# x's causal convolution taken in token rows instead of channel columns, in a hybrid Mamba-2 and attention layer

## The reference, cut to what matters

```
def causal_depthwise_conv(u, w, b):
    k = w.shape[0]
    out = lax.conv_general_dilated(u, w[:, None, :], (1,), padding=[(k - 1, 0)], feature_group_count=u.shape[-1])
    return out + b

xbc = silu(causal_depthwise_conv(xbc, conv_w, conv_b))
xs, Bm, Cm = split(xbc)
y = ssd_chunked(xs, dt, A, Bm, Cm)
y = y + d_skip * xs
y = group_rms_norm(y * silu(z)) * norm_w
```

## Time and profile before

| | |
|---|---|
| median of three runs | 2049.8 us |
| profiled execution: its time | 2051.72 us |
| profiled execution: span, first to last instruction | 2050.1 us |
| busy share: TensorE, VectorE, ScalarE, GpSimd | 100%, 76%, 57%, 8% |
| DMA traffic | 419.80 MB, 205 GB/s mean |

### The profile page before, as it was taken

One profiled execution on the slowest core, in us unless ns is written; L12 is line 12 of the kernel. 1 busy time (PEld: TensorE's weight loads), 2 busy tenths in 40 slices (PEclk: granted clock), 3 DMA queues, 4 the chain that ended last, 5 costly groups with the idle time before them and its releaser, 6 DMA issues.

```text
span 2050.1 us, 28075 instructions
## 1 busy us (share of the span) xinstructions
PE 2040.8 (100%) x9580; PEld 1677.7 (82%) x9580; DVE 1566.3 (76%) x1861; ACT 1172.0 (57%) x1496; POOL 171.6 (8%) x195
## 2 busy tenths in 40 slices
PE   9999999999999999999999999999999999999999
PEld 8888877778888888888888888888888888887887
DVE  6777866665856777777667887888898889877866
ACT  5444655555556666666655554556666666645543
POOL 1121000000011222222000000010000000000000
PEclk9999999999999999999999999999999999999999
DMA  7656675654566666666565657598888888667574
GB/s 250 199 182 203 188 220 166 176 162 152 182 204 186 185 185 184 185 190 187 167 192 183 212 168 238 177 307 244 258 254 237 250 259 250 196 205 232 176 246 154
DMA packets 220626, 419.80 MB, mean 205 GB/s; under 512 B 16449, under 2 KB 22002, under 8 KB 220290
## 3 DMA queue, kind: packets, MB, share of 16 engines
q1 hardware_dynamic: 212162, 399.48, 61.8%
q0 software_dynamic: 7776, 18.94, 4.4%
q10 hardware_dynamic: 608, 0.34, 0.1%
HBM read 410.25 MB, written 4.26 MB: 202 GB/s over the span
## 4 chain that ended last, share of the span: by engine, by line
PE 92%; DVE 3%; DMA 2%; ACT 1%; issue 0%; SPq 0%; DVEq 0%; ACTq 0%
PE acc L2246 72%; PE side L2333 8%; PE acc L2333 6%; PE side L2262 3%; DMA w_raw<-in_w_ffn_down 1%; DVE w_lo L2038 1%; PE side L2402 1%; PE side L2549 1%; DVE w_raw L1953 0%; ACT w_hi L1216 0%; DVE w_lo L1257 0%; DMA x_row<-in_x 0%; DMA w_raw<-in_w_in 0%; PE acc L2262 0%; ACT w_hi L724 0%
## 5 line engine op out<-in xcount | busy, mean ns | idle before, releaser
L1257 DVE TENSOR_TENSOR w_lo<-w_raw,w_hi 128x1024 fp32r<-128x1024 f32 x332 | 420.7, 1280 | 245.7 <-ACT w_hi L724 244.5
L724 ACT ACTIVATE w_hi<-w_raw 128x1024 fp32r<-128x1024 f32 x332 | 348.5, 1057 | 355.7 <-PE acc L2246 315.2
L2246 PE MATMUL acc<-w_hi,h_hi 128*128 128x512 f32 x1248 | 498.7, 400 | 0.2
L2246 PE MATMUL acc<-w_hi,h_lo 128*128 128x512 f32 x1248 | 487.0, 390 | 0.0
L2246 PE MATMUL acc<-w_lo,h_hi 128*128 128x512 f32 x1248 | 485.9, 389 | 0.0
L2246 PEld LDWEIGHTS acc<-w_hi,h_hi 128*128 128x128 f32 x1248 | 234.4, 188 | 52.7 <-issue 7.0
L2246 PEld LDWEIGHTS acc<-w_hi,h_lo 128*128 128x128 f32 x1248 | 234.3, 188 | 50.3
L2246 PEld LDWEIGHTS acc<-w_lo,h_hi 128*128 128x128 f32 x1248 | 234.7, 188 | 47.6 <-issue 1.9
L1932 DVE TENSOR_TENSOR w_lo<-w_raw,w_hi 128x1024 fp32r<-128x1024 f32 x136 | 165.1, 1220 | 38.0 <-ACT w_hi L1137 35.4
L1053 ACT ACTIVATE w_hi<-w_raw 128x1024 fp32r<-128x1024 f32 x110 | 116.6, 1061 | 117.2 <-PE acc L2246 70.2
L1137 ACT ACTIVATE w_hi<-w_raw 128x1024 fp32r<-128x1024 f32 x136 | 142.9, 1057 | 65.8 <-PE acc L2246 50.4
(11 more groups left out here) (436 smaller groups left out, 3445.9 us busy)
## 6 DMA issues: line engine op xcount, KB each, us to landing
w_raw<-in_w_in SPq DMA_DIRECT2D x320, 512.0 KB, 4.3
w_raw<-in_w_ffn_down SPq DMA_DIRECT2D x88, 512.0 KB, 4.9
w_raw<-in_w_ffn_gate SPq DMA_DIRECT2D x68, 512.0 KB, 4.6
w_raw<-in_w_ffn_up SPq DMA_DIRECT2D x68, 512.0 KB, 5.2
w_raw<-in_w_ssm_proj SPq DMA_DIRECT2D x64, 512.0 KB, 4.4
side_raw<-in_w_ffn_up SPq DMA_DIRECT2D x40, 512.0 KB, 4.7
w_raw<-in_w_attn_proj SPq DMA_DIRECT2D x32, 512.0 KB, 3.7
w_raw<-in_w_out SPq DMA_DIRECT2D x32, 512.0 KB, 4.7
```

What stands on the lines that cost most here:

```text
L724: nc.scalar.activation(w_hi[:, r], w_raw[:, n % RING], ACT.Copy).then_inc(hi_ready, 1)
L1257: nc.vector.tensor_tensor(w_lo[:, r], w_raw[:, n % RING], w_hi[:, r].bitcast(F32), ALU.subtract).then_inc(lo_ready, 1)
L2246: done = nc.tensor.matmul(acc[p][:, t], a[:, k0 + kk, cut], w[:, r, kk], start=first and kk == n == 0, stop=last and kk == UK - 1 and n == ...
```

## The change

x stays in token rows. SyncE copies `x_proj` three times inside SBUF, shifted by one, two and three partitions (tokens), into `earlier[0..2]`; of each, a second small copy carries the one, two or three tokens that cross from the first token tile to the second. These six copies are issued ahead of the load of z7. GpSimd loads the group's taps and bias, broadcast to all partitions (1 MB and 256 KB). VectorE multiplies four tiles by taps (after z6 and z7), adds them and the bias (after x0' and x1'), ScalarE does the SiLU in place after x2', and VectorE computes `xdt` and `xdt_end` after x4' of the next x chunk. TensorE's sixteen transposes per group and ScalarE's four first taps and `y_row` copy are gone. `y_products` moves from after x1' to after x2', `y_rows` from after x3' to after x4', the scaling of `y_row` moves from VectorE to ScalarE, `exps` to ScalarE's steps 4 and 5, the d_skip product stands behind the loads of the next group on GpSimd and reads `x_proj`.

```diff
         x_proj = at("x_proj", 187, [P, TT, CW])
-        conv_x = at("conv_x", 191, [P, CT, T])
+        earlier = [at(f"earlier{n + 1}", kb, [P, TT, CW]) for n, kb in enumerate((138, 142, 175))]
+        taps_b = at("taps_b", 167, [P, TAPS, CW])
...
+                for u in range(UPC):
+                    if u == UPC - 1:
+                        sp.wait_ge(x_rows_ready, i + 1)
+                        for back in range(1, TAPS):
+                            sp.dma_start(earlier[back - 1][back:P], x_proj[0:P - back]).then_inc(shift_in, 16)
+                            sp.dma_start(earlier[back - 1][0:back, 1], x_proj[P - back:P, 0]).then_inc(shift_in, 16)
+                    load(w_in, u * UK, (i + i) * (CW // 2) + COL_Z)
             with repeat(sp, 2, [(unit, 2 * UPC)]) as i:
                 for c in range(2):
...
+                act.wait_ge(conv_ready, g + 1)
+                nc.scalar.activation(x_proj[:], x_proj[:], ACT.Silu).then_inc(xs_ready, 1)
+            def tail_normed(g):
+                act.wait_ge(y_rstd, g + 1)
+                for t in range(TT):
+                    last = nc.scalar.activation(y_row[:, t], y_row[:, t], ACT.Copy, scale=y_scale[:, t:t + 1])
+                last.then_inc(y_ready, 1)
             def tail_columns(g):
...
+                    act.wait_ge(xdt_ready, g)
+                    act.wait_ge(skip_ready, g)
                 for t in range(TT):
                     last = nc.scalar.activation(x_proj[:, t], acc[0][:, t], ACT.Copy, scale=x_rstd[:, t:t + 1])
                 last.then_inc(x_rows_ready, 1)
+                act.wait_ge(x_rows_ready, g + 1)
+                nc.scalar.sem_inc(acc_free[0], 1)
             def exps(g, hf, head):
                 act.wait_ge(acs_masked, g * 2 + (hf + 1))
+                if hf == 0:
+                    act.wait_ge(taps_read, g + 1)
                 if hf == 0 and not head:
...
-                        act.wait_ge(x_T, g + 1)
-                        for n in range(CT):
-                            last = conv_first_taps(sums(0)[:, n], g * CT, conv_x[:, n], n)
-                        last.then_inc(conv_first, 1)
                     if u == 1:
                         act.wait_ge(cb_sum, g + 1)
                         nc.scalar.activation(cb[:], side[:, 0, 0:3 * P], ACT.Copy).then_inc(cb_ready, 1)
-                    if u == 2:
-                        act.wait_ge(conv_done, g + 1)
-                        nc.scalar.activation(conv_x[:], conv_x[:], ACT.Silu).then_inc(xs_ready, 1)
-                        exps(g, 0, head)
-                    if u == 3:
-                        exps(g, 1, head)
-                    if u == 5:
-                        act.wait_ge(xdt_ready, g + 1)
-                        nc.scalar.activation(y_row[:], side[:, 2:4], ACT.Copy).then_inc(xrow_ready, 1)
+                    if u == 0 and not head:
+                        tail_normed(g - 1)
+                    if u in (4, 5):
+                        exps(g, u - 4, head)
+                    if u == 6:
+                        conv_silu(g)
                 chunk_done()
...
+            def by_taps(tile, back):
+                return nc.vector.tensor_tensor(tile[:], tile[:], taps_b[:, TAPS - 1 - back].unsqueeze(1).broadcast_to([P, TT, CW]), ALU.mult)
+            def conv_step(g, u):
+                if u == 2:
+                    dve.wait_ge(shift_in, g * 96 + 96)
+                    dve.wait_ge(taps_in, g * 32 + 32)
+                    by_taps(earlier[0], 1)
+                    by_taps(earlier[1], 2)
+                if u == 3:
+                    by_taps(earlier[2], 3)
+                    by_taps(x_proj, 0).then_inc(taps_read, 1)
+                if u == 4:
+                    dve.wait_ge(taps_read, g + 1)
+                    nc.vector.tensor_tensor(earlier[0][:], earlier[0][:], earlier[1][:], ALU.add)
+                    link(nc.vector.tensor_tensor(x_proj[:], x_proj[:], earlier[2][:], ALU.add))
+                if u == 5:
+                    link(nc.vector.tensor_tensor(x_proj[:], x_proj[:], earlier[0][:], ALU.add))
+                    nc.vector.tensor_tensor(x_proj[:], x_proj[:], conv_bias_b[:].broadcast_to([P, TT, CW]), ALU.add).then_inc(conv_ready, 1)
+            def x_scaled(g):
                 by_head = "p (h d) -> p h d"
+                dve.wait_ge(xs_ready, g + 1)
+                for t in range(TT):
+                    last = nc.vector.tensor_tensor(
+                        xdt[:, t].rearrange(by_head, d=HP), x_proj[:, t].rearrange(by_head, d=HP),
+                        dt[:, t, bass.ds(g * HG, HG)].unsqueeze(2).broadcast_to([P, HG, HP]), ALU.mult)
+                last.then_inc(xdt_ready, 1)
+                dve.wait_ge(xdt_ready, g + 1)
+                nc.vector.tensor_tensor(
+                    xdt_end[:].rearrange(by_head, d=HP), xdt[:, 0].rearrange(by_head, d=HP),
+                    edge[:, 0, bass.ds(g * HG, HG)].unsqueeze(2).broadcast_to([P, HG, HP]), ALU.mult).then_inc(xdt_end_ready, 1)
+            def tail_step(g, u):
+                if u == 0:
+                    x_scaled(g)
+                if u == 4:
+                    tail_gated(g)
+            def x_chunk(g, head):
                 for u in range(UPC):
                     split_lo()
-                    if u == 0:
-                        dve.wait_ge(conv_first, g + 1)
-                        for back in range(1, TAPS):
-                            conv_taps(g, back)
-                    if u == 1 and not head:
+                    if not head:
+                        tail_step(g - 1, u)
+            def z_chunk(g, head):
+                for u in range(UPC):
+                    split_lo()
+                    if u == 2 and not head:
                         tail_transposed(g - 1)
-                    if u == 2:
-                        dve.wait_ge(conv_done, g + 1)
-                        nc.vector.sem_inc(acc_free[0], 1)
-                    if u == 3:
-                        decays(g, 0)
-                    if u == 4:
-                        decays(g, 1)
-                    if u == 5:
-                        dve.wait_ge(xs_T, g + 1)
-                        for t in range(TT):
-                            last = nc.vector.tensor_tensor(
-                                xdt[:, t].rearrange(by_head, d=HP), side[:, 2 + t].rearrange(by_head, d=HP),
-                                dt[:, t, bass.ds(g * HG, HG)].unsqueeze(2).broadcast_to([P, HG, HP]), ALU.mult)
-                        last.then_inc(xdt_ready, 1)
-                        dve.wait_ge(xdt_ready, g + 1)
-                        if head:
-                            dve.wait_ge(edge_ready, 1)
-                        nc.vector.tensor_tensor(
-                            xdt_end[:].rearrange(by_head, d=HP), xdt[:, 0].rearrange(by_head, d=HP),
-                            edge[:, 0, bass.ds(g * HG, HG)].unsqueeze(2).broadcast_to([P, HG, HP]), ALU.mult).then_inc(xdt_end_ready, 1)
+                    conv_step(g, u)
+                    if u in (6, 7):
+                        decays(g, u - 6)
             x_chunk(0, True)
+            dve.wait_ge(edge_ready, 1)
             z_chunk(0, True)
             with repeat(dve, G - 1, [(unit, 2 * UPC), (own, conv_links)]) as i:
                 x_chunk(i + 1, False)
...
+            def taps_load(g):
+                ours = conv_w[0][:, bass.ds(g * CW, CW)]
+                pool.dma_start(taps_b[:], ours.partition_broadcast(P)).then_inc(taps_in, 16)
+                pool.dma_start(conv_bias_b[:], conv_b[:, bass.ds(g * CW, CW)].partition_broadcast(P)).then_inc(taps_in, 16)
...
+            def skip(g, first=False):
                 by_head = "p (h d) -> p h d"
-                pool.wait_ge(xrow_ready, g + 1)
+                pool.wait_ge(xs_ready, g + 1)
+                if not first:
+                    pool.wait_ge(y_T, g)
                 for t in range(TT):
-                    x_heads = y_row[:, t].rearrange(by_head, d=HP)
                     last = nc.gpsimd.tensor_tensor(
-                        x_heads, x_heads, d_skip_b[:, bass.ds(g * HG, HG)].unsqueeze(2).broadcast_to([P, HG, HP]), ALU.mult)
+                        y_row[:, t].rearrange(by_head, d=HP), x_proj[:, t].rearrange(by_head, d=HP),
+                        d_skip_b[:, bass.ds(g * HG, HG)].unsqueeze(2).broadcast_to([P, HG, HP]), ALU.mult)
                 last.then_inc(skip_ready, 1)
...
+            def next_group(i, first=False):
                 pool.wait_ge(decay_exp, i * 2 + 2)
                 loads(i + 1)
+                skip(i, first)
+                pool.wait_ge(y_sum, i + 1)
+                taps_load(i + 1)
                 tail(i)
-                group(i + 1)
+                masks(i + 1)
+            next_group(0, True)
+            with repeat(pool, G - 2, [(own, 2)]) as i:
+                next_group(i + 1)
+            skip(G - 1)
...
             def tail_between(g):
                 def between(u):
-                    if u == 1:
```

(83 more changed lines are left out.)

35 lines of the change are left out of this document (11 added, 24 removed).

## The result

The changed kernel takes 2258.85 us as the median of four runs (2252.52 to 2260.68), the one before beside it 2049.65 us: a ratio of 1.1012, 95% interval [1.0988, 1.1036]. It is 209 us slower; 171 us slower were forecast.

What follows compares the result with a forecast made beforehand. TensorE was taken to bound the kernel. Per group, 23.4 us lost to late copies less 2.05 for transposes gives 21.4; eight groups add 171, so 2221 us; own bounds 2199 to 2251, range 2150 up to 2290 to 2310.

Steps and rivals of the forecast that it cites:

- What bounded it, and the possible gain: TensorE, busy nearly throughout; dropping its transposes could save 2.05 us a group, 16.4 us in all, 0.8%.
- The copies on one engine: Shifted copies of x_proj: equal shares of whole rows put 666 KB on one DMA engine, 27.5 us; few engines had 0.84.
- The landing: Copies all in earlier, 31.8 us after x7's end (30.5 to 33.5); VectorE stands still for 18 us.
- SyncE's issues: Six copy issues of 0.37 us on SyncE delay z7's load by 2.2 us, which four slots cover.
- The chain behind the landing: VectorE and ScalarE work from the copies' arrival to xdt, 23.5 us; y_products then starts at 55.3 instead of 31.9.
- s: The time at which the shifted copies have landed, from which the steps up to xdt were counted.
- 4 us more: After the wait at z7, TensorE also stands for xdt this long, which hides a slow unit or two.
- The clock: TensorE's possible 1.2 GHz level after the wait: taken as nothing, up to 8 us a group, 64 in all, kept for the range.
- The sum: Eight groups lose 21.4 us each, 171 in all: 2223 us, or 2221 against the median.
- The third rival: One engine and a slow clock or slower single-engine copy: 2270 to 2290 us; chance 0.1, counted within few engines' 0.84.
- even copies: Copies spread evenly land at about 8 us, but xdt is 4.6 us late for y_products: 2071 us; chance 0.09.
- The full gain of the transposes: Even copies and xdt ready by 31.9 us, so the transposes' time is simply gained: 2033 us; chance 0.05.

Runs made afterwards that it cites:

- the best version: Changed kernel, all copies cut, tail two units later, copies issued three, two, one, first exps released after two products, d_skip's product held until xdt_end is written: 2051.9 us.
- the cut run: Changed kernel with each shifted copy cut in two, 112 partition rows and the remaining 15, 14 or 13: 2097.3 us, ratio 1.0206.
- GpSimd's queue: Changed kernel with the six whole copies issued by GpSimd after its masks instead of by SyncE: 2141.0 us in a single run.
- the matmuls of no use: Changed kernel, whole copies, with 58 idle matmuls ahead of z7 and 20 ahead of y_products: 2240.1 us in a single run.
- the run kept busy: Changed kernel with all copies cut, plus 20 idle matmuls of 512 columns ahead of y_products: 2080.6 us, ratio 1.0139.
- the later tail: Changed kernel with all copies cut, y_products after x4', y_rows after x6', gating, squares, scaling and y_columns moved to match: 2068.9 us, ratio 1.0076.

## Why the prediction was right, point by point

**What bounded it, and the possible gain:** held as far as it was shown. The transposes' 16.4 us are not seen by themselves in any run; the best version (1.0005) ends where the kernel before was, with late remainders as the likely cause.

**The copies on one engine:** right, and the runs show it from three sides (share 0.06, the cut run, GpSimd's queue). The landing was put 29.6 us after `x_proj`; it was 31.2 in the group shown (772.83 to 803.99), so at 33.4 after x7's end instead of 31.8. That group is the quickest of the eight: the others landed at 33.8 to 35.3, the mean is 34.1, and the bounds of 30.5 to 33.5 were too low for seven of them. 666 KB in 31.2 less issue and fixed part (0.7 and 1.7, the second an assumption) are 23.1 KB/us, at the low end of the 22.9 to 25.4 from the earlier trace rows; by the mean they are 22.6.

**SyncE's issues:** wrong in size and without effect on the sum. Six issues of 0.37 us were priced at 2.2 us. Already the first took 0.67, SyncE was held for 8.85 us at the first small copy and 4.27 at the last, and z7's load went out 16.6 us after the first copy. It was there about when the copies were (rounded at 805.13), as it would be if a part of it had to pass the same engine, so the two waits lay beside each other as forecast.

**The chain behind the landing:** right. From s to `xdt` 23.5 us were worked out, and 22.9 measured (803.99 to 826.9; 22.7 in the mean); `y_products` began 56.3 us after x7's end, worked out as 55.3. The second wait, 4.49 us, was named as "4 us more" in the part on the clock.

**The clock:** one of the two terms that were mis-sized, with the landing. I took nothing and kept 8 us a group for the range. The granted clock was 0.50 behind both waits (by single microseconds from 827 to 829 behind the second). The first slow stretch lies under VectorE's chain; the second has nothing to hide it, `y_products` took 3.26 us for 32 matmuls instead of 1.97, and from there to x7's end 18.9 us passed where 17.0 stood in the sum. With the matmuls of no use it is 2.2 us a group.

**The sum:** 21.4 us a group forecast. From the group times 76.4 - 50.8 = 25.6 were measured, 8 x 25.6 = 205 of the 209; the other 4 lie ahead of the first group. In the mean of the groups the copies landed 2.3 us later than forecast (34.1 for 31.8), the chain to `xdt` was 0.8 shorter, and from there to x7's end 19.6 us passed where 17.0 stood: 2.3 - 0.8 + 2.6 = 4.1, the difference of the forecast's group of 72.3 and 76.4. With the matmuls of no use the last stretch is 17.8 us, so some 2 of the 2.6 are the clock. So the mechanism was right and two sizes too small. The 2259 us lie above the 2251 that the forecast's own bounds give; that they lie in the range is owed to the width kept for the clock and a slow copy. The third rival named both, at 2270 to 2290; the truth lies between it and the forecast. Two smaller signs were off as well: the group was 76 us and not 72, and the DMA share in it 0.55 and not 0.45.

**The rivals:** even copies were forecast at 2071 with the late `xdt`, 21 us above the kernel before; the cut run is this rival's mechanism, with `xdt` at 36.5 in the group read, and lies 43 above it. Its price left out the clock (some 2 us a group by the run kept busy) and small waits for remainders. The full gain of the transposes (2033) was reached by no version, though in the last one the late `xdt` and the clock's fall are gone and the copies are waited for 10 us in all.

The Trainium skill, TensorE: Matmul & The Clock Gate, section "HAM oscillation — how this bites in real kernels", says that waits for DMA bring the clock down each time they come; the trace agrees, with 0.50 in the first wait of all eight groups.

## What to carry to other kernels

Before a copy goes to a queue, ask whether the count of its rows can be shared out: the copies with the one of 127 rows landed 31 us after `x_proj`, the same rows cut in 112 and the rest about 11. Where a change takes work from the bounding engine and lays a dense stretch on the one that feeds it, write both down on one clock: the gain counts only if each hand-over of the stretch comes before it is asked for. And a wait of the bounding engine can cost more than its length: here some 2 us a group at the lower clock behind it.

## What the runs showed of the hardware that I had not expected

SyncE is held at the issue of a small copy of 2 KB for 8.5 to 9.6 us while the copy of 127 rows before it is under way, in each of the eight groups; with that copy cut the same issue took 0.6 to 1.8 us. So a slow copy can delay the issue of what follows, and not only its landing. The same 127 rows from GpSimd's queue land in 6.6 us. Behind a wait of 4.5 us before `y_products` the granted clock was 0.50 for about 3 us, behind one of 3.2 us before z7 too, and in three groups of the later tail behind one of 1.8 to 1.9 us. And 20 matmuls that count for nothing in the first of these waits made the kernel 15 us faster. GpSimd's product of 3.9 us stretched one VectorE instruction in each half of it from 1.22 to 2.07 us, and took 3.9 us itself where it took 3.0 in the run with the later tail; holding it back by some ten microseconds gave 3 to 4 us in all.
